# A hybrid decoder step on one core: fetch-aligned TensorE loops, an earlier turn of the next tile, and another bank for the group maps

## The chip, the core and the metric

The kernel runs on one core of a Trainium2 chip. The metric is the device time of one execution in microseconds (us), the median over several runs. TensorE (PE in the rows; PEld is its loading of weights) multiplies, VectorE (DVE) and ScalarE (ACT) do elementwise work, GpSimd (POOL) issues the indirect DMAs and SyncE (SP) most of the others. Each engine has a sequencer that runs its own stream of instructions (PEldq in the rows is TensorE's). Matrix products accumulate in eight banks of PSUM, here `ps[:, 0..7, :]`.

## What is computed

One layer over 1,024 prompt tokens and 64 sample tokens, all in float32, D = 1024:

```python
h = rmsnorm(x, norm1_g)
proj = h @ w_in                                  # u, v, p: 512 columns each
u, v = gelu(proj[..., :512]), layernorm(gelu(proj[..., 512:1024]))
p = proj[..., 1024:]
ya = u * (tril(W_s[h]) @ v_chunk + b[h])         # 4 heads, chunks of 128 tokens
yb = (window_mean(p, 2/4/8/16) - p) @ b_w[g] * b_scale   # 4 groups of 128
x = x + concat(ya, yb) @ w_out
h2 = rmsnorm(x, norm2_g)
eidx, gates = hier_route(h2, ...)                # best of 4 groups, then 2 of its 8 experts
x = x + moe_ffn(h2, eidx, gates, w1, w3, w2)     # 32 SwiGLU experts, 1024 -> 512 -> 1024
y = rmsnorm(x, normf_g)
```

## The kernel before

**The trunk.** `pipeline` runs `step(i, cur, prev, pprev, nxt)` over nine tiles of 128 tokens (i = 0 to 8; the last, "sample", has 64). Steps 2 to 6 are a hardware loop, the others are written out. Every engine has its own `step`, and semaphores tie them together; within an engine the order is the order of the code. On TensorE a step makes these things in a row: the v products (L1249, bank 2), the p products (L1258, bank 4), the u products (L1258, bank 3), the spatial products z (L1274, bank 5), the turn (transposition) of the next tile's normalised `xn` into banks 0 and 1 (L1199), the group maps `bw` of the pooling branch (L1308, bank 6), the turn of the tile before for the router (L1199, banks 0 and 1 again), the first half of the output product (L1326, bank 6), the router's logits (L1334), the second half (L1342, bank 7). `hT` is what VectorE makes of the next tile's turn (`take_hT`, L842): it scales banks 0 and 1 into SBUF. It may only do so when the p and u products, which read the old `hT`, are done, and the router's turn waits for it, since it writes the same banks. `xT_done`, `hT_ready`, `yaT_ready`, `ybT_ready` and `yb_done` are the semaphores in between: `yT` has the four heads' part ("ya") in its first four slices and the groups' part ("yb") in its last four.

On VectorE a step adds the output halves of the tile before, normalises, makes `v`, the pooled sums `poolT` (`pool_tile`), then adds the bias to z (L1010), multiplies by u (L1014, gives `yaT_ready`), makes `hT` (L842), and scales the maps (L1031, gives `ybT_ready`). In step 7 (`LAST - 1`) TensorE also turns the last 15 rows of the pooling input into bank 4 (L1280) and ScalarE copies them out (L726, gives `rows_copied`).

**The experts.** 32 blocks, one an expert, in triples: `triples` writes out the first three blocks (the first triple), then runs a hardware loop for triples 1 to 6 (block sizes 96, 80, 64 tokens), a second loop for triples 7 to 9 (80, 80, 64), and writes out the last two blocks. A block of TensorE (`block_triple`) has 128 products with the two up matrices, four chunks of weights of 1 MB each (L1372, 256 records in the trace, each with a weight load of its own), the turn of the next block's rows (L1199, 8 records), and eight products with the down matrix, two chunks (L1393, 16 records). SyncE loads each chunk of a later triple into the place of the chunk that TensorE has just used (`used`, L470); 18 chunks are held, so a load is asked for one triple ahead. Both loops lie behind one another in TensorE's instruction stream with one register instruction between them; line 346 is the loop's own control on each engine.

TensorE's instructions are fetched in blocks of 256 (16 KB); in the trace they are the packets of DMA queue q8, the instruction queue.

Of the kernel before, what the change touches and what calls it, by code (L numbers as in the profile page):

```python
# [14 lines left out]
P = 128  # L15
# [8 lines left out]
HEADS = GROUPS = 4  # L24
STATE = 15
WINDOWS = (2, 4, 8, 16)
HALO = 16
NG, NE, EPG = 4, 32, 8
NR = NG + NE
FE = 512  # L30
# [35 lines left out]
def reached(eng, sem, n):  # L66

    if not isinstance(n, int) or n > 0:
        eng.wait_ge(sem, n)
# [7 lines left out]
def build(nc, x_prompt, x_sample, state_pool, norm1_g, w_in, a_norm_g, a_norm_b, ws_sht, bs_th,  # L77
# [4 lines left out]
    with ctx:  # L82
# [253 lines left out]
        def m_of(kind):  # L336
            return NS if kind == "sample" else P
# [4 lines left out]
        def triples(eng, block_triple):  # L342

            block_triple(0, (CAP,) * SETS)
            for lo, hi, caps_of in CLASSES:
                with eng.Fori(lo, hi) as h:
                    block_triple(h, caps_of)
            block_triple(FINAL, FINAL_CAPS)
# [459 lines left out]
        def _(dve):  # L808
# [29 lines left out]
            def take_hT(i, m):  # L838
                dve.wait_ge(xT_done, i + 1)
                reached(dve, proj_p, i)  # L840
                reached(dve, proj_u, i)
                dve.tensor_tensor(hT[:, :, 0:m], wide[:, :, 0:m],  # L842
                                  g1t[:, :].unsqueeze(2).to_broadcast([P, KD, m]), ALU.mult)\
                    .then_inc(hT_ready, 1)
# [87 lines left out]
            def step(i, cur, prev, pprev, nxt):  # L932
# [73 lines left out]
                    dve.wait_ge(share_step, 7)  # L1006
                if cur and cur != "sample":
                    pool_tile(i, cur == "first")
                    dve.wait_ge(z_done, i + 1)
                    dve.tensor_tensor(ya[:, :], ps[:, 5, :], bias.rearrange("p h n -> p (h n)"), ALU.add).then_inc(z_biased, 1)  # L1010
                    dve.wait_ge(z_biased, i + 1)
                    dve.wait_ge(u_gelu, i + 1)
                    reached(dve, out_b, i)
                    dve.tensor_tensor(yT[:, 0:HEADS, :], ya.rearrange("p (h n) -> p h n", n=P),  # L1014
                                      u.rearrange("p (h n) -> p h n", n=P), ALU.mult).then_inc(yaT_ready, 1)
                if cur == "sample":
# [5 lines left out]
                        last = dve.scalar_tensor_tensor(ya[0:m, c], ps[0:m, 5, c], bst_s[0:m, h:h + 1],  # L1022
                                                        u[0:m, c], ALU.add, ALU.mult)
                    last.then_inc(ya_ready, 1)
                if nxt:
                    take_hT(i + 1, m_of(nxt))
                if cur:
                    m = m_of(cur)
                    dve.wait_ge(yb_done, i + 1)
                    reached(dve, out_b, i)  # L1030
                    dve.tensor_tensor(yT[:, HEADS:KD, 0:m],  # L1031
                                      ps[:, 6, :].rearrange("p (g n) -> p g n", n=P)[:, :, 0:m],
                                      bsc[:, :].unsqueeze(2).to_broadcast([P, GROUPS, m]), ALU.mult)\
                        .then_inc(ybT_ready, 1)
                if prev:
# [158 lines left out]
        def _(pe):  # L1194
            def turn(x, m, done, k=KD, bank=0, whole=False):

                xs = x[0:m, :].rearrange("t (k p) -> t k p" if whole else "t (p k) -> t k p", k=k)
                for c in range(k):
                    last = pe.transpose(ps[:, bank + c // 4, (c % 4) * P:(c % 4) * P + m], xs[:, c, :],  # L1199
                                        ident[0:m, 0:m])  # L1200
                last.then_inc(done, 1)
# [25 lines left out]
            def step(i, cur, prev, pprev, nxt):  # L1227
# [9 lines left out]
                if cur:  # L1237
                    m = m_of(cur)
                    pe.wait_ge(hT_ready, i + 1)
                    if cur == "sample":  # L1240
                        pe.wait_ge(rows_copied, 1)
                        half_tile_projections(i)
                    else:
                        reached(pe, v_gelu, i)
                        reached(pe, logits_ready, i - 1)
                        for k in range(KD):
                            if isinstance(i, int) and i == 0 and k % 2 == 0:
                                pe.wait_ge(in_win[k // 2], 16)
                            last = pe.matmul(ps[:, 2, :], hT[:, k, :], win[:, k, AW:2 * AW],  # L1249
                                             start=(k == 0), stop=(k == KD - 1))  # L1250
                        last.then_inc(proj_v, 1)
                        for bank, part, free, done in ((4, 2, p_copied, proj_p), (3, 0, u_gelu, proj_u)):
                            reached(pe, free, i)
                            for j in range(AW // P):
                                for k in range(KD):
                                    for c in range(SPLIT):
                                        at = part * AW + j * P + c * NS
                                        last = pe.matmul(ps[c * NS:(c + 1) * NS, bank, j * P:(j + 1) * P],  # L1258
                                                         win[:, k, at:at + NS], hT[:, k, :], start=(k == 0),
                                                         stop=(k == KD - 1), skip_group_check=True)  # L1260
                            last.then_inc(done, 1)
# [21 lines left out]
                    if cur == "sample":  # L1283
# [7 lines left out]
                                                     src[0:kk, g * P + c * w:g * P + (c + 1) * w], bnd[0:kk, g, 0:m],  # L1291
                                                     start=(n == 0), stop=(n == 1), skip_group_check=True)
                        last.then_inc(pooled, 1)
                if nxt:
                    pe.wait_ge(xn_ready, i + 2)
                    reached(pe, h2T_ready, i - 1)
                    turn(xn, m_of(nxt), xT_done)
                if cur:
                    m = m_of(cur)
                    if cur == "sample":  # L1300
                        pe.wait_ge(ya_ready, 1)
                        turn(ya, m, yaT_done, HEADS, 5, whole=True)
                    pe.wait_ge(poolT_ready, i + 1)
                    reached(pe, x2a_ready, i)
                    w = P // SPLIT if cur == "sample" else P
                    for g in range(GROUPS):
                        for c in range(P // w):
                            last = pe.matmul(ps[c * w:(c + 1) * w, 6, g * P:g * P + m], bw[:, g, c * w:(c + 1) * w],  # L1308
                                             poolT[:, g, 0:m], start=True, stop=True, skip_group_check=True)
                    last.then_inc(yb_done, 1)  # L1310
                if prev:
# [4 lines left out]
                if cur:  # L1316
                    m = m_of(cur)
                    if isinstance(i, int) and i == 0:
                        pe.wait_ge(in_wout, 32)
                    pe.wait_ge(yaT_ready, i + 1)  # L1320
                    pe.wait_ge(ybT_ready, i + 1)
                    if cur == "sample":
                        half_tile_output(range(2))
                    else:
                        for k in range(KD):
                            last = pe.matmul(ps[0:m, 6, :], yT[:, k, 0:m], wout[:, k, 0:512],  # L1326
                                             start=(k == 0), stop=(k == KD - 1))
                        last.then_inc(out_a, 1)
# [173 lines left out]
```

## Time and profile before

| | us |
|---|---|
| median of 3 runs | 975.38 (974.15 to 977.6) |
| profiled execution | 981.15 |
| its span, first to last instruction | 979.4 |
| TensorE busy | 888.5 (91%) |
| VectorE busy | 280.8 (29%) |
| TensorE, trunk (to the last router product) | 8.3 to 386.1 |
| TensorE, experts | 390.7 to 943.6 |
| final norm and output behind it | to 979.4 |

The mean granted clock of TensorE over the span was 0.964 of full speed. A row of a timeline has the start in us from the span's start, how long the group lasted, the engine, the source line, the operation, its tiles and shapes, how often, and in brackets the idle time before it and what ended it. "issue" there means that nothing the profile shows was waited for.

### The profile page before, as it was taken

The numbers are of one execution on the slowest core, as the hardware profiler recorded it, in microseconds if no ns is written. First come the engines' busy times: TensorE is split into PE (matmuls) and PEld (weight loads), VectorE is DVE, ScalarE is ACT, GpSimd is POOL, SyncE is SP. The second block draws the span as 40 slices with busy tenths as digits, with TensorE's granted clock in tenths as the row PEclk, the third lists the DMA queues.
The fourth block names the chain that finished last, engine by engine and source line by source line (L and its number), as shares of the span: only waits on it lengthen the run. The fifth ranks groups of instructions, "written<-read, shape, count | busy, mean of one in ns | idle before, by whom it ended". The sixth has DMA issues, their size and how long they took to land. (4 is left out here: it accounts for less than half of the span.)

```text
span 979.4 us, 28026 instructions
## 1 busy us (share of the span) xinstructions
PE 888.5 (91%) x12186; PEld 641.1 (65%) x12186; DVE 280.8 (29%) x838; ACT 100.9 (10%) x158; POOL 155.3 (16%) x262
## 2 busy tenths in 40 slices
PE   4899999999999994999999899997999999999940
PEld 2766848667585762778677576776676767777630
DVE  2544555645556355330101001010010101010106
ACT  0110100101001011010010000000101010101014
POOL 1000100000000002122131302221221322222110
PEclk9999999999999996899999899999999999999985
DMA  9770210201011047999999999999999999999628
GB/s 336 260 271 1 88 39 4 86 0 43 21 64 44 3 140 274 398 400 377 370 399 396 395 370 378 409 389 406 359 396 403 392 407 392 406 395 405 249 68 321
DMA packets 57407, 258.42 MB, mean 264 GB/s; under 512 B 10633, under 2 KB 11713, under 8 KB 40436
## 3 DMA queue, kind: packets, MB, share of 16 engines
q1 hardware_dynamic: 47436, 237.98, 60.9%
q0 software_dynamic: 9264, 19.36, 8.0%
q8 instruction: 56, 0.92, 0.4%
q10 hardware_dynamic: 640, 0.07, 0.1%
q14 instruction: 11, 0.09, 0.0%
HBM read 240.33 MB, written 25.04 MB: 271 GB/s over the span
## 5 line engine op out<-in xcount | busy, mean ns | idle before, releaser
L1372 PEld LDWEIGHTS ps<-hT,big 128*64 128x64 f32 x8192 | 300.1, 139 | 47.1 <-issue 44.7
L1372 PE MATMUL ps<-hT,big 128*64 128x80 f32 (+2 forms) x8192 | 309.8, 236 | 18.2 <-issue 15.1
L1393 PE MATMUL ps<-big,poolT 128*80 128x512 f32 (+2 forms) x512 | 191.2, 594 | 0.6 <-issue 0.6
L1146 DVE TENSOR_TENSOR poolT<-u,ps 128x320 f32<-128x320 f32 (+2 forms) x32 | 15.6, 486 | 427.1 <-PE ps L1372 427.1
L1393 PEld LDWEIGHTS ps<-big,poolT 128*80 128x80 f32 (+2 forms) x512 | 64.5, 150 | 103.1 <-issue 102.0
L1258 PEld LDWEIGHTS ps<-hT,big 128*64 128x64 f32 x2048 | 111.6, 137 | 6.1 <-issue 6.1
L1258 PE MATMUL ps<-hT,big 128*64 128x128 f32 x2048 | 113.6, 273 | 0.0
L584 POOL DMA_INDIRECT x_rows<-xn,sidx x22 | 32.7, 1487 | 278.1 <-ACT xn L782 268.3
L561 POOL DMA_INDIRECT slot_table<-ids,dest x18 | 18.8, 1042 | 300.6 <-DVE dest L899 297.5
L1249 PE MATMUL ps<-big,hT 128*128 128x512 f32 x128 | 58.9, 611 | 4.2 <-DMA big<-in_w_in 2.8
L1326 PE MATMUL ps<-big 128*128 128x512 f32 x128 | 56.4, 593 | 2.1 <-DVE big L1031 2.1
L1342 PE MATMUL ps<-big 128*128 128x512 f32 x128 | 57.0, 598 | 0.0
L782 ACT ACTIVATE xn<-ps,gslot 80x1024 f32<-80x1024 f32 (+1 forms) x21 | 23.3, 1110 | 260.1 <-PE ps L1393 247.8
L1249 PEld LDWEIGHTS ps<-big,hT 128*128 128x128 f32 x128 | 24.3, 195 | 33.4 <-issue 26.7
L1326 PEld LDWEIGHTS ps<-big 128*128 128x128 f32 x128 | 23.7, 190 | 29.2 <-issue 29.0
L1342 PEld LDWEIGHTS ps<-big 128*128 128x128 f32 x128 | 23.7, 190 | 27.6 <-issue 27.3
L1199 PE MATMUL ps<-ident,xn 128*128 128x128 f32 (+1 forms) x144 | 20.5, 289 | 18.6 <-DVE xn L836 8.3
L1063 DVE TENSOR_TENSOR hT<-ps,g2t 128x768 f32<-128x768 f32 (+1 forms) x32 | 28.0, 875 | 27.6 <-PE ps L1199 18.8
L579 POOL DMA_INDIRECT gslot<-gate_rows,pidx x32 | 32.2, 1007 | 21.1 <-POOL sidx L630 13.3
L1199 PEld LDWEIGHTS ps<-ident,xn 128*128 128x128 f32 (+1 forms) x144 | 18.0, 194 | 20.0 <-issue 15.2
L584 POOL DMA_INDIRECT x_rows<-bands,sidx x10 | 14.6, 1460 | 92.6 <-DVE bands L1153 79.4
L703 ACT ACTIVATE xn<-big 128x1024 f32 (+2 forms) x9 | 9.5, 1057 | 171.9 <-DVE big L969 171.9
(202 smaller groups left out, 564.8 us busy)
## 6 DMA issues: line engine op xcount, KB each, us to landing
big<-in_exp_w SPq DMA_DIRECT2D x192, 1024.0 KB, 11.1
big<-in_w_in SPq DMA_DIRECT2D x4, 1536.0 KB, 12.7
big<-in_w_out SPq DMA_DIRECT2D x2, 2048.0 KB, 16.3
x_rows<-big SPq DMA_DIRECT2D x8, 512.0 KB
h_rows<-xn SPq DMA_DIRECT2D x8, 512.0 KB, 2.9
big<-x_rows SPq DMA_DIRECT2D x8, 512.0 KB, 6.9
out_y_prompt<-big SPq DMA_DIRECT2D x8, 512.0 KB, 2.8
big<-in_x_prompt SPq DMA_DIRECT2D x1, 3072.0 KB, 11.2
```

The costliest lines, as they stand in the source:

```text
L561: pool.indirect_dma_start(slot_table, bass.IndirectOffsetOnAxis(ap=dest[0:m, j, c:c + 1], axis=0), ids[0:m, j, c, :], None, bounds_check=N ...
L579: pool.indirect_dma_start(dst, None, gate_rows, bass.IndirectOffsetOnAxis(ap=idx.bitcast(U32), axis=0), bounds_check=last_pair, oob_is_err ...
L584: pool.indirect_dma_start(x3_rows, bass.IndirectOffsetOnAxis(ap=idx.bitcast(U32), axis=0), src, None, bounds_check=last_row, oob_is_err=Tr ...
L782: act.activation(ys[s][0:m, :], ps[0:m, 5:7, :].rearrange("p a n -> p (a n)"), ACT.Copy, scale=gslot[s][0:m, 0:1]).then_inc(y_ready, 1)
L1063: dve.tensor_tensor(xT[:, :, 0:ways * i].rearrange("p k (w i) -> p k w i", i=i), wide.rearrange("p k (i w) -> p k w i", w=WAYS)[:, :, 0:wa ...
L1199: last = pe.transpose(ps[:, bank + c // 4, (c % 4) * P:(c % 4) * P + m], xs[:, c, :], ident[0:m, 0:m])
L1249: last = pe.matmul(ps[:, 2, :], hT[:, k, :], win[:, k, AW:2 * AW], start=(k == 0), stop=(k == KD - 1))
L1258: last = pe.matmul(ps[c * NS:(c + 1) * NS, bank, j * P:(j + 1) * P], win[:, k, at:at + NS], hT[:, k, :], start=(k == 0), stop=(k == KD - 1 ...
L1326: last = pe.matmul(ps[0:m, 6, :], yT[:, k, 0:m], wout[:, k, 0:512], start=(k == 0), stop=(k == KD - 1))
L1342: last = pe.matmul(ps[0:m, 7, :], yT[:, k, 0:m], wout[:, k, 512:D], start=(k == 0), stop=(k == KD - 1))
L1372: last = pe.matmul(out[c * w:(c + 1) * w, j, 0:m], up_weights(n)[:, k, j * P + c * w:j * P + (c + 1) * w], xT[:, 4 * half + k, 0:m], start ...
L1393: last = pe.matmul(ps[first:first + m, 5 + cols, :], hhT[:, 2 * half + k, 0:m], down_weights(n)[:, k, cols * 512:(cols + 1) * 512], start= ...
```

## The change

Three edits. First, on TensorE alone each of the two expert loops begins on a boundary of 256 instructions; the space to the boundary is filled with NOPs, which are executed on the way in (none is skipped by a branch). Second, the turn of the next tile stands between the p and the u products, and on VectorE `take_hT` stands ahead of the bias and the product with u. Third, the group maps of the full tiles go to bank 4, not 6 (which takes a wait for `rows_copied` in step 7), and the first half of the output product waits for `ybT_ready` only ahead of its fifth slice.

```diff
+FETCH_BLOCK = 256
...
             for lo, hi, caps_of in CLASSES:
+                if eng is nc.tensor:
+                    eng.addr_align(FETCH_BLOCK)
                 with eng.Fori(lo, hi) as h:
                     block_triple(h, caps_of)
...
                     pool_tile(i, cur == "first")
+                    if nxt:
+                        take_hT(i + 1, m_of(nxt))
                     dve.wait_ge(z_done, i + 1)
...
-                if nxt:
-                    take_hT(i + 1, m_of(nxt))
...
-                                      ps[:, 6, :].rearrange("p (g n) -> p g n", n=P)[:, :, 0:m],
+                                      ps[:, 6 if cur == "sample" else 4, :].rearrange("p (g n) -> p g n", n=P)[:, :, 0:m],
...
                         for bank, part, free, done in ((4, 2, p_copied, proj_p), (3, 0, u_gelu, proj_u)):
+                            if bank == 3 and nxt:
+                                pe.wait_ge(xn_ready, i + 2)
+                                reached(pe, h2T_ready, i - 1)
+                                turn(xn, m_of(nxt), xT_done)
                             reached(pe, free, i)
...
-                if nxt:
-                    pe.wait_ge(xn_ready, i + 2)
-                    reached(pe, h2T_ready, i - 1)
-                    turn(xn, m_of(nxt), xT_done)
...
+                    maps = 6 if cur == "sample" else 4
+                    if isinstance(i, int) and i == LAST - 1:
+                        pe.wait_ge(rows_copied, 1)
...
-                            last = pe.matmul(ps[c * w:(c + 1) * w, 6, g * P:g * P + m], bw[:, g, c * w:(c + 1) * w],
+                            last = pe.matmul(ps[c * w:(c + 1) * w, maps, g * P:g * P + m], bw[:, g, c * w:(c + 1) * w],
...
                     pe.wait_ge(yaT_ready, i + 1)
-                    pe.wait_ge(ybT_ready, i + 1)
                     if cur == "sample":
+                        pe.wait_ge(ybT_ready, i + 1)
                         half_tile_output(range(2))
                     else:
                         for k in range(KD):
+                            if k == HEADS:
+                                pe.wait_ge(ybT_ready, i + 1)
                             last = pe.matmul(ps[0:m, 6, :], yT[:, k, 0:m], wout[:, k, 0:512],
```

TensorE in the trunk's loop, from the p products to the first output half, before. A name behind "waits" is a semaphore; `ps<-ident,xn` is a turn.

```order
47 L1258 MATMUL ps<-hT,big 64x128 [waits p_copied]
48 L1258 MATMUL ps<-hT,big 64x128 x63
49 L1258 MATMUL ps<-hT,big 64x128 [waits u_gelu]
50 L1258 MATMUL ps<-hT,big 64x128 x63
51 L1274 MATMUL ps<-done_early,v 128x128 [waits rank_taken,v_ready]
52 L1274 MATMUL ps<-done_early,v 128x128 x3
53 L1295 REGISTER_ALU
54 L1199 MATMUL ps<-ident,xn 128x128 [waits h2T_ready,xn_ready]
55 L1199 MATMUL ps<-ident,xn 128x128 x7
56 L1308 MATMUL ps<-poolT,done_early 128x128 [waits x2a_ready,poolT_ready]
57 L1308 MATMUL ps<-poolT,done_early 128x128 x3
58 L1199 MATMUL ps<-ident,xn 128x128 [waits hT_ready,x2n_ready]
```

The same place on TensorE in the changed kernel (its lines are numbered 3 to 8 higher).

```order
53 L1265 MATMUL ps<-hT,big 64x128 x63
54 L1257 REGISTER_ALU
55 L1202 MATMUL ps<-ident,xn 128x128 [waits h2T_ready,xn_ready]
56 L1202 MATMUL ps<-ident,xn 128x128 x7
57 L1265 MATMUL ps<-hT,big 64x128 [waits u_gelu]
58 L1265 MATMUL ps<-hT,big 64x128 x63
59 L1281 MATMUL ps<-done_early,v 128x128 [waits rank_taken,v_ready]
60 L1281 MATMUL ps<-done_early,v 128x128 x3
61 L1314 MATMUL ps<-poolT,done_early 128x128 [waits x2a_ready,poolT_ready]
62 L1314 MATMUL ps<-poolT,done_early 128x128 x3
63 L1202 MATMUL ps<-ident,xn 128x128 [waits hT_ready,x2n_ready]
```

The eight transpositions of the next tile stand ahead of the 64 u products, and between z and the router's turn only the four group maps are left.

VectorE in the same loop, before: bias, product with u, `hT`, scaling of the maps.

```order
212 L1010 TENSOR_TENSOR big<-ps,gf 128x512 [waits z_done]
213 L1014 TENSOR_TENSOR big<-big,u 128x512 [waits out_b,u_gelu,z_biased]
214 L842 TENSOR_TENSOR hT<-ps,g1t 128x1024 [waits proj_u,proj_p,xT_done]
215 L1031 TENSOR_TENSOR big<-ps,bsc 128x512 [waits out_b,yb_done]
```

VectorE there in the changed kernel.

```order
212 L845 TENSOR_TENSOR hT<-ps,g1t 128x1024 [waits proj_u,proj_p,xT_done]
213 L1015 TENSOR_TENSOR big<-ps,gf 128x512 [waits z_done]
214 L1019 TENSOR_TENSOR big<-big,u 128x512 [waits out_b,u_gelu,z_biased]
```

`hT` stands first, and the two operations that make the heads' part of `yT` come behind it.

## Rows read from the trace of the kernel before

**Rows 1.** TensorE's waits: line waited for: us in total, times, longest.

```profile
PE ps L1199 <- DVE hT L842: 5.8, 6, 1.0
```

**Rows 2.** Timeline of TensorE, tile 3, maps and router's turn.

```profile
163.37 1.06 PE L1308 MATMUL ps<-poolT,done_early 128*128 128x128 f32 x8
165.38 1.13 PE L1199 MATMUL ps<-ident,xn 128*128 128x128 f32 x8 [0.96 <-DVE hT L842]
```

**Rows 3.** Timeline of VectorE, tile 3: next tile's norm, bias, product, hT.

```profile
146.82 0.75 DVE L836 TENSOR_SCALAR xn<-big,ss 128x1024 f32 x1 [0.17 <-DVE ss L827]
...
162.69 0.69 DVE L1010 TENSOR_TENSOR big<-ps,gf 128x512 f32<-128x512 f32 x1 [4.21 <-PE ps L1274]
163.41 0.69 DVE L1014 TENSOR_TENSOR big<-big,u 128x512 f32<-128x512 f32 x1
164.02 1.22 DVE L842 TENSOR_TENSOR hT<-ps,g1t 128x1024 f32<-128x1024 f32 x1
```

**Rows 4.** Timeline of TensorE, tile 0: p and u products, maps, output.

```profile
23.50 14.19 PE L1258 MATMUL ps<-hT,big 128*64 128x128 f32 x256
...
40.57 1.16 PE L1308 MATMUL ps<-poolT,done_early 128*128 128x128 f32 x8 [0.91 <-DVE poolT L928]
43.82 7.11 PE L1326 MATMUL ps<-big 128*128 128x512 f32 x16 [2.09 <-DVE big L1031]
```

**Rows 5.** Timeline of VectorE, tile 0: norm of tile 1.

```profile
30.69 0.75 DVE L836 TENSOR_SCALAR xn<-big,ss 128x1024 f32<-128x1024 f32 x1
```

**Rows 6.** Timeline of TensorE, tile 7: maps and router's turn without a wait.

```profile
330.13 1.16 PE L1308 MATMUL ps<-poolT,done_early 128*128 128x128 f32 x8
331.12 1.08 PE L1199 MATMUL ps<-ident,xn 128*128 128x128 f32 x8
```

**Rows 7.** Timeline of ScalarE, tile 7: the copy that gives rows_copied.

```profile
329.27 0.59 ACT L726 ACTIVATE xg<-ps 16x512 f32<-16x512 f32 x1 [1.52 <-PE ps L1280]
```

**Rows 8.** Windows of the experts: stretch, length, busy us (records), PEclk, DMA share, GB/s.

```profile
551.46:574.82 23.36, 17.98 (x274) 14.99 (x273) 1.65 (x2) 1.17 (x2) 4.00 (x6) 0.78 1.02 401
502.50:516.64 14.14, 14.14 (x273) 11.74 (x273) 1.65 (x2) 1.17 (x2) 4.03 (x6) 1.00 1.02 399
659.89:681.34 21.45, 16.39 (x274) 13.24 (x273) 1.65 (x2) 1.17 (x2) 4.01 (x6) 0.92 1.02 406
...
599.89:609.88 9.99, 8.54 (x258) 7.95 (x257) 0.00 (x0) 1.49 (x2) 4.05 (x6) 1.00 1.02 378
650.24:658.81 8.57, 8.31 (x258) 7.86 (x257) 0.00 (x0) 1.49 (x2) 4.02 (x6) 1.00 1.02 383
706.45:716.15 9.70, 8.58 (x257) 8.01 (x256) 0.00 (x0) 1.49 (x2) 4.04 (x6) 1.00 1.03 380
```

**Rows 9.** Loop control of TensorE's sequencer, whole run: ns min/median/max, first and last start.

```profile
L346 PEldq COMPARE_BRANCH  x9: 76/222/7127, 502.6 to 909.9; - x9
...
L346 PEldq MOVE  x2: 29/32/34, 448.7 to 766.5; - x2
```

**Rows 10.** The same control at 551 to 553 us.

```profile
L346 PEldq ALU_OP  x1: 32/32/32, 551.5 to 551.5; - x1
L346 PEldq COMPARE_BRANCH  x1: 7127/7127/7127, 551.6 to 551.6; - x1
```

**Rows 11.** Instruction packets, 506 to 555.1 us (triple 2): packets, MB, share.

```profile
q8 instruction: 1, 0.02, 0.2%
```

**Rows 12.** The same from 555.1 to 614.4 us (triple 3).

```profile
q8 instruction: 8, 0.13, 0.9%
```

**Rows 13.** Timeline of TensorE: first products of triples 1, 3 and 7.

```profile
455.74 10.78 PE L1372 MATMUL ps<-hT,big 128*64 128x96 f32 x256
...
559.08 4.10 PE L1372 MATMUL ps<-hT,big 128*64 128x96 f32 x47 [3.97 <-issue]
...
769.72 9.48 PE L1372 MATMUL ps<-hT,big 128*64 128x80 f32 x256
```

**Rows 14.** SyncE's chunk loads, 866 to 890 us: issue to landing.

```profile
DMA to landing us min/median/max: 25.1/25.1/25.1
```

## The prediction

> **What bounds the kernel now.** Read TensorE's line first: it is busy 91% of the span, so what counts is where it waits and what it executes. Its list of waits names one wait that recurs in the trunk, on `hT`, six times and 5.8 us in all [rows 1]. In the experts it has no large wait with a releaser at all; what is left there is called "issue". The timeline shows where: 3.97 us of nothing ahead of the first product of triple 3 [rows 13], and no such gap at the start of triple 2. Windows laid from the down products of one triple to the first turn of the next give 14.14 us into triple 2, 23.36 into triple 3 and 21.45 into triple 5 [rows 8]. The records are the same (273 or 274), so 9.2 and 7.3 us are pure loss. Part is idle time and part a slow TensorE: the granted clock is 0.78 and 0.92 of full in these windows, against 1.00.
>
> The sequencer's rows say what the gap is. Its nine loop branches take 222 ns in the median, the worst 7,127 ns [rows 9]; that one starts at 551.6 us [rows 10] and ends at 558.7, just ahead of the product at 559.08. The queue of instruction packets fits: one packet in all of triple 2, eight in triple 3 [rows 11, 12]. So triple 2 ran from instructions that were still there, and triple 3 had to fetch its body again, its first block at the branch itself, while TensorE ran dry.
>
> **Why it alternates.** A triple is 3 x (256 + 8 + 16) = 840 products, each with a weight load: 1,680 instructions, and some 13 for control and waits, 1,693 or 6.6 blocks of 256. In triple 3 the products stop again after 47 [rows 13]: 94 instructions and about four others, so the loop's head lies some 98 instructions short of a boundary. 98 + 6 x 256 = 1,634, so 59 more lie in an eighth block. I take it that eight blocks are kept: when a triple runs wholly from kept ones, the fetch of a ninth at its end drops the first, and the back edge misses. Then all come in again in a row, the last too late as well: the third block of triples 3 and 5 lasts 9.99 and 9.70 us where the same products last 8.57 in triple 4 [rows 8]. Loop 2 is the control. It starts 59 + 1 instructions into that eighth block, so it touches only seven, and its back edges are among the seven branches that don't stall [rows 9].
>
> **The loops aligned.** From a boundary, 1,693 instructions touch seven blocks, with the next one eight. What goes: 9.2 + 7.3 us at the two back edges and 1.4 + 1.1 us in the two third blocks, **19.0 us**. Loop 2 gains nothing, it fits already.
>
> What comes is the padding, executed once at each entry: about 98 + 4 = 102 NOPs ahead of loop 1 (the trunk's edits take a few wait instructions out in front of it) and 1,792 - 1,693 - 1 = 98 ahead of loop 2. They hide behind the down products queued in TensorE. At loop 1 the sequencer is at the head at 448.7 us [rows 9], TensorE needs the next product at 455.74 [rows 13], and from a branch's end to the product took 559.08 - 558.7 = 0.4 us: cover 6.7 us. At loop 2 it is there at 766.5, needed at 769.72 (a block of 64 tokens has half as long down products): cover 2.8 us. No NOP is in the trace. The floor is a register move's own 32 ns [rows 9], the ceiling the 100 ns from the start of one control instruction to the next, 551.5 to 551.6 [rows 10], which has the recording of it in it. I take 60 ns, nearer the floor since in the timed runs nothing is recorded. Loop 1: 6.1 us, hidden. Loop 2: 5.9 us, of which 3.1 us TensorE idles, and I add 1.2 us for a clock that may drop after it: the gap of 3.97 and a second of 1.41 us came with 9.2 us of loss, so 3.8 us beyond idling. **Cost 4.3 us.** At 32 ns: 3.3 and 3.1 us, cost 0.3. At 100 ns: 3.5 + 7.0 us idle and twice 3.8, cost 18.1.
>
> **A rule that speaks against this.** The branch that ends triple 1 took some 0.2 us and the one that ends triple 2 took 7.1 [rows 9, 10], with one packet in triple 2 [rows 11]; so a jump of 1,693 instructions back can find its target. The Trainium skill ("Runtime: NRT & Kernel Launch", "Instruction fetch mechanics") says that a taken branch whose target lies outside a window of two pages forces a fetch before execution goes on. By that rule every back edge of both loops would stall in both kernels, and the aligning would bring nothing; the trace disagrees at seven of nine branches. It is a rival below.
>
> **The turn moved ahead of the u products.** The eight transpositions are the same in number, so only the wait goes. From the maps to the router's turn is 165.38 - 163.37 = 2.01 us in tile 3 [rows 2] and 331.12 - 330.13 = 0.99 where nothing is waited for [rows 6]: 1.0 us a tile. `xn` is ready at 147.6 [rows 3], and the p products end at about 154.4, so the turn doesn't wait in the loop. The new order on VectorE: `hT` can start when the u products end, about 162.5 on the shifted clock, and takes 1.2 us; then bias and product, 0.72 and 0.69 us from start to start and end [rows 3], done at 165.2. TensorE's maps and router's turn are through at 165.4. So the output product finds `yT` ready by 0.2 us; if the chain is that much longer, as much comes back. I count 0.95 us, and the wait occurs six times: **5.7 us**. The scaling of the maps is now late, but the output product asks for it only at its fifth slice, 1.8 us on.
>
> Tile 0: p ends at 23.50 + 7.1 = 30.6 [rows 4], `xn` of tile 1 comes at 31.4 [rows 5], so the moved turn waits 0.8 us. It is given back: the maps waited 0.91 us for `poolT` anyway and start where they did, 40.57. Behind them `hT` (1.2), bias and product (1.4) run from 40.6 to 43.2, against 43.82 before: **+0.6 us**. Tile 7: the maps now wait for ScalarE's copy of 0.59 us, which begins 0.1 us after the products it reads [rows 7]; formerly the next tile's turn lay in between and covered it. Maps later by **0.8 us**. Other tiles need no new wait for bank 4: `poolT` is made from what was copied out of it. The trunk is worth 5.7 + 0.6 - 0.8 = **5.5 us**, and since TensorE leads into the routing chain, everything behind it comes as much earlier.
>
> **Is anything late next?** The weights. SyncE loads a chunk when its predecessor is used; in triple 9 it took 25.1 us to land [rows 14], with the DMA engines full [rows 8]. If all 19 us that the stalls gave the queue are added, 44.1 us; it is needed one triple (47.4 us) less its own use (2.7 us) later, 44.7. It fits even then, and the queue was partly idle in the stalls, so the true figure is lower.
>
> **Sum.** 19.0 - 4.3 + 5.5 = 20.2 us. The profiled execution, 981.15, goes to 961.0; the runs' median lies 5.8 us below it, so **955.2 us**.
>
> **Rivals.** (1) Dear NOPs, at or near 100 ns: gain 19.0 + 5.5 - 18.1 = 6.4, **969.0 us**; for it, the only spacing that the trace has; against it, that spacing includes recording. (2) The aligning does not cure the misses, by the two-page rule or since the head doesn't land where it should: the trunk's 5.5 less 0 to 4.3 for the NOPs, **970 to 974 us**. Against it: loop 2. (3) The weights bind in triple 9 and the last two blocks: the margin above is 0.6 us at its worst, and a miss would cost some 3 us, **958 us**. (4) Slower: the NOPs alone decide. With both covers used up (9.5 us) and 7.6 us of slow clock, 200 NOPs cost 200c - 1.9 us; over 24.5 + 2.9 us, that is from c = 0.146 us on. At 0.16 us each the kernel takes 30.1 - 24.5 = 5.6 us longer, **981 us**. A move's own 32 ns speaks against it.
>
> **How the numbers follow.** Forecast 0.66 (951 to 961, both ends from the NOP's price), dear NOPs 0.14, no cure 0.10, weights 0.07, slower 0.03. The range takes in forecast, weights and nearly all of the dear NOPs: low 949.5 (NOPs free, 24.5 us, and 1.4 us less in the first pass of loop 1, whose third block, too, fetches), high 968. About 0.3%, 2.9 us, is what a measurement can tell from no change: faster 0.93 (the no-cure case lies at or under 972.5 in six cases of ten), same 0.04, slower 0.03.
>
> **What would show it.** Right: all loop branches of TensorE near 0.2 us; no instruction packets in triples 3 to 6; windows of 14.1 us into triples 3 and 5; clock 1.00 through the experts; router's turn 1.0 us behind the maps. The gap at 769.72 on the new clock prices the NOP. Wrong: a branch of microseconds, a gap over 4 us at loop 2 or any at loop 1, an output product that waits for the product with u, or products of the last triple that wait for a chunk.

## The result, and the profile after

The changed kernel takes 960.18 us (median of four runs, 958.86 to 961.16) against 974.76 us of the kernel before in the same comparison: ratio 0.9846 with a 95% interval of 0.9819 to 0.9873, 1.5% or about 15 us faster. The forecast was 955.2 us, in a range of 949.5 to 968. The profiled execution took 959.59 us, 957.9 of it its span, with a mean granted clock of 0.967.

The long back edges are gone. TensorE's sequencer rows for the loop's own line (min, median and max duration in ns), which answer to [rows 9]:

```profile
L349 PEldq ALU_OP  x9: 32/32/32, 501.4 to 888.7; - x9
L349 PEldq COMPARE_BRANCH  x9: 76/208/233, 501.5 to 888.9; - x9
```

The worst of nine branches takes 233 ns, where it was 7,127. The windows into triples 2, 3 and 5, then the third block of triple 3 (length, busy time of each engine, clock, DMA share, GB/s), answer to [rows 8]:

```profile
501.60:515.79 14.19, 14.19 (x274) 11.79 (x273) 1.69 (x3) 1.17 (x2) 4.03 (x6) 1.00 1.02 397
549.18:563.33 14.15, 14.15 (x274) 11.75 (x273) 1.65 (x2) 1.17 (x2) 4.01 (x6) 1.00 1.02 398
...
644.72:658.86 14.14, 14.14 (x273) 11.74 (x273) 1.65 (x2) 1.17 (x2) 4.01 (x6) 1.00 1.03 394
592.61:600.23 7.62, 7.62 (x138) 5.35 (x136) 1.38 (x2) 0.01 (x1) 2.36 (x4) 1.00 1.03 373
```

All are alike, at full clock, and TensorE is busy from end to end. The queue of instruction packets moves 39 in all (56 before), and none between 502.2 and 751.9 us; the DMA groups of the page and its row for the weights:

```profile
q8 instruction: 39, 0.64, 0.3%
...
big<-in_exp_w SPq DMA_DIRECT2D x192, 1024.0 KB, 21.5
```

A chunk of weights lands 21.5 us after its issue in the median.

The NOPs are in the trace, unlike before, and so have a price. Sequencer rows of the aligning line:

```profile
L348 PEldq NOP  x200: 13/13/13, 445.9 to 747.6; - x100
```

Their starts are 102 from 445.87 to 453.33 and 98 from 740.50 to 747.55: (747.55 - 740.50) / 97 = 72.7 ns from one to the next (73.9 at loop 1), though each lasts 13. TensorE's timeline at the two entries (start, length, engine, line, operation, tiles, count, idle time before):

```profile
445.95 7.03 PE L1401 MATMUL ps<-big,poolT 128*96 128x512 f32 x16
453.97 1.21 PE L1380 MATMUL ps<-hT,big 128*64 128x96 f32 x24 [0.99 <-issue]
...
740.25 3.65 PE L1401 MATMUL ps<-big,poolT 128*64 128x512 f32 x16
748.02 10.78 PE L1380 MATMUL ps<-hT,big 128*64 128x80 f32 x254 [4.12 <-issue]
760.36 0.35 PE L1380 MATMUL ps<-hT,big 128*64 128x80 f32 x2 [1.55 <-issue]
```

At loop 1 TensorE misses the first product by 0.99 us, at loop 2 by 4.12 us. The block behind the second gap takes 10.78 us where one of 80 tokens takes 9.1, since the granted clock is half of full for 3.4 us after it; and its last two products come 1.55 us late, after an instruction packet that moved at 757.8 us. In the trunk, tile 3:

```profile
145.83 7.21 PE L1265 MATMUL ps<-hT,big 128*64 128x128 f32 x128
152.97 1.16 PE L1202 MATMUL ps<-ident,xn 128*128 128x128 f32 x8
154.06 7.21 PE L1265 MATMUL ps<-hT,big 128*64 128x128 f32 x128
161.20 1.16 PE L1281 MATMUL ps<-done_early,v 128*128 128x128 f32 x8
162.19 1.06 PE L1314 MATMUL ps<-poolT,done_early 128*128 128x128 f32 x8
163.08 1.05 PE L1202 MATMUL ps<-ident,xn 128*128 128x128 f32 x8
164.01 6.28 PE L1334 MATMUL ps<-big 128*128 128x512 f32 x14
```

The router's turn stands 0.89 us behind the maps, no longer 2.01 [rows 2]. Tiles 0 and 7:

```profile
31.97 1.16 PE L1202 MATMUL ps<-ident,xn 128*128 128x128 f32 x8 [1.25 <-DVE xn L839]
...
43.69 7.11 PE L1334 MATMUL ps<-big 128*128 128x512 f32 x16 [1.45 <-DVE big L1019]
...
326.82 1.13 PE L1314 MATMUL ps<-poolT,done_early 128*128 128x128 f32 x8 [0.83 <-ACT xg L729]
```

### The profile page after: what moved, and what is told of

Its sections match the earlier page's. It is cut to its first block and busy times, and to the rows that moved or that the text cites. A ratio compares the mean times of both kernels' runs of the same rounds, so it can differ in the third digit from the quotient of the medians.

```text
span 957.9 us, 28219 instructions
## 1 busy us (share of the span) xinstructions
PE 879.2 (92%) x12186; PEld 634.2 (66%) x12186; DVE 280.1 (29%) x838; ACT 100.8 (11%) x158; POOL 155.3 (16%) x262
## 5 line engine op out<-in xcount | busy, mean ns | idle before, releaser
L1380 PEld LDWEIGHTS ps<-hT,big 128*64 128x64 f32 x8192 | 292.5, 139 | 37.0 <-issue 35.4
L1380 PE MATMUL ps<-hT,big 128*64 128x80 f32 (+2 forms) x8192 | 297.9, 235 | 12.5 <-issue 11.5
L1265 PEld LDWEIGHTS ps<-hT,big 128*64 128x64 f32 x2048 | 111.5, 137 | 7.0 <-issue 6.1
L1202 PEld LDWEIGHTS ps<-ident,xn 128*128 128x128 f32 (+1 forms) x144 | 18.0, 194 | 15.8 <-issue 9.5
## 6 DMA issues: line engine op xcount, KB each, us to landing
big<-in_exp_w SPq DMA_DIRECT2D x192, 1024.0 KB, 21.5
```

The lines of the kernel that those rows point to most:

```text
L1380: last = pe.matmul(out[c * w:(c + 1) * w, j, 0:m], up_weights(n)[:, k, j * P + c * w:j * P + (c + 1) * w], xT[:, 4 * half + k, 0:m], start ...
```

## The experiments

The first four ran on one chip, where the kernel before took 973.47 us (median of seven runs, 971.74 to 975.06).

**The kernel before, recorded again.** No edit.

> The kernel before, unchanged, for a second profile of it. In the first, the 64-token blocks of TensorE took 8.6 us where the changed kernel's take 7.6, with three short stops in each, also in triples that fetched no instructions; and the profiled execution was 5.8 us over the median of the runs. If those stops belong to that one recording, this profile shows 64-token blocks of 7.6 us, an execution near 975 us, and the same two long branches (6 to 7 us) ahead of triples 3 and 5. If they belong to the kernel (where its loops lie in the instruction stream), the blocks take 8.6 us again.

Measured: 973.93 us, span 971.8. Windows into triples 3 and 5, and the third block of triple 5:

```profile
552.66:573.81 21.15, 16.47 (x273) 13.41 (x272) 1.65 (x2) 1.17 (x2) 4.00 (x6) 0.92 1.03 404
...
657.40:679.33 21.93, 15.94 (x274) 13.05 (x273) 1.65 (x2) 1.17 (x2) 4.01 (x6) 0.92 1.03 404
...
704.25:713.75 9.50, 7.83 (x257) 7.68 (x257) 0.00 (x0) 1.49 (x2) 4.03 (x6) 1.00 1.02 382
```

Against windows of 14.15 us into triples 2 and 4 of the same trace, the back edges lose 7.0 and 7.8 us; against 7.62 us of the changed kernel the third blocks lose 1.3 and 1.9. Together about 18 us: the misses and their price repeat. Two things differ from the first recording. A block of 64 tokens takes 7.7 us here, not 8.6 [rows 8], and a triple 1.2 us less (609.75 to 657.52 against 611.08 to 660.01 from branch to branch), so that the first recording's span was longer by 7.6 us. And TensorE's clock falls in tile 0, behind the wait of 2.10 us there, so that sixteen products which take 7.11 us at [rows 4] take 8.80:

```profile
43.55 8.80 PE L1326 MATMUL ps<-big 128*128 128x512 f32 x16 [2.10 <-DVE big L1031]
```

**Only the aligning.**

```diff
+                if eng is nc.tensor:
+                    eng.addr_align(FETCH_BLOCK)
```

> Only the aligning of the two loops; the trunk as before. Theory (eight fetch blocks are kept, an aligned triple touches seven): all nine loop branches of TensorE near 0.2 us, no instruction packets in triples 3 to 6, and of the 14.6 us that the whole change brought some 9, so about 966 us. The NOPs, 71 ns each in the changed kernel's trace, cost what they cost there: a gap of 1 us at loop 1 and 4.1 us at loop 2. Rival (the trunk's new order moved the loop's code or relieved the weights, and the aligning does nothing by itself): 975 us, with the long branches still there.

Measured: 965.09 us (963.87 to 966.28), ratio 0.9907 (0.9887 to 0.9926), 9.1 us less by that ratio, 8.4 between the medians. All branches are short (233 ns at most); 197 NOPs run. The gap at loop 2 has the same size, but the half clock behind it lasts 6.8 us here, and in tile 0, too (sixteen products in 10.1 us):

```profile
754.93 11.48 PE L1375 MATMUL ps<-hT,big 128*64 128x80 f32 x254 [4.12 <-issue]
```

So the aligning alone removes some 18 us and returns half of them.

**Only the trunk's edits.** The changed kernel without the two lines above.

> Only the trunk's edits (turn ahead of the u products, hT first on VectorE, maps in bank 4); no aligning. Theory: 5.5 us less than before, about 969.3 us, the expert loops with their long branches ahead of triples 3 and 5 as before. The changed kernel's trace has 0.70 us less a tile than before in tiles 2 to 6 (40.69 against 41.39), not the 0.95 that I counted, and the first router product of tile 8 came 3.6 us earlier: by that rival reading the trunk is worth 3.6 us, 971.2 us.

Measured: 967.37 us (966.57 to 968.98), ratio 0.9931 (0.9913 to 0.9949), 6.7 us less by the ratio, 6.1 between the medians. The misses stay, with their second stop after 49 products now, not 47 (the new order has three instructions fewer in front of the loop, which took 102 NOPs to align, where the old one took 99; its body reaches 56 instructions into the eighth block, not 59):

```profile
553.90 3.92 PE L1378 MATMUL ps<-hT,big 128*64 128x96 f32 x49 [2.73 <-issue]
559.32 5.50 PE L1378 MATMUL ps<-hT,big 128*64 128x96 f32 x128 [1.50 <-issue]
```

9.1 and 6.7 make 15.8; the two parts add up within the intervals. By one pair of traces, the first recording of before and the changed kernel, the trunk's edits bring 3.6 us where the order before didn't lose its clock, and more where it did: the product that ranks the last tile, the end of the trunk, starts at 385.1, 386.5 and 388.3 us in three recordings with the old order, with 0, 3.4 and 6.8 us of half clock in tile 0, and at 381.6 and 381.9 in the changed kernel and this one, with none. None of the eleven recordings with the new order, those below among them, shows a drop in tile 0: their clock stays at 1.00 from about 18 to 357 us at least. TensorE's longest idle time there is 1.4 us now instead of 2.1, which had 0.5 to 1.1 us of idling just ahead of it. That may be the reason, but it isn't shown: it wasn't tried by itself, the first recording idled 0.9 + 2.1 us and kept its clock, and the wait ahead of the moved turn, up to 1.5 us, is new. And four of the eleven lose the clock later instead, for 3.4 us from 357 or 358 us on, which none of the three with the old order does. One of them, the next kernel below, starts its last ranking at 383.2 us. Why it falls there is open.

**The padding jumped over.** `addr_align` may end in a branch to the boundary instead of NOPs.

```diff
-                    eng.addr_align(FETCH_BLOCK)
+                    eng.addr_align(FETCH_BLOCK, max_nops=0)
```

> The changed kernel, but the padding ahead of both loops is jumped over by one branch, so that none of the 200 NOPs is executed. Theory: the NOPs' gaps of 1.0 and 4.1 us and the 3.4 us of half clock behind the second (1.7 us) go, 6 to 7 us, so about 953.5 us. Rival: the jump leaves the blocks that were fetched in order, so the loop's first block must be fetched at the branch itself, as at the long branches of before: 3 to 4 us of gap at each loop, and the kernel stays at 960 or goes to 963 us.

Measured: 956.87 us (956.11 to 960.16), ratio 0.9824 (0.9806 to 0.9842). The two jumps take 1,999 and 288 ns and neither leaves a gap, and the clock stays at 1.00 from 399 to 925 us. But against the ratio of the changed kernel only some 2 us are gained, of the 6 to 7 that the two gaps and the slow clock had cost. TensorE's timeline in the last triples says where they went in the one execution recorded:

```profile
883.56 1.94 PE L1401 MATMUL ps<-big,poolT 128*64 128x512 f32 x8 [1.22 <-DMA big<-in_exp_w]
886.39 1.94 PE L1401 MATMUL ps<-big,poolT 128*64 128x512 f32 x8 [0.90 <-DMA big<-in_exp_w]
888.98 7.33 PE L1380 MATMUL ps<-hT,big 128*64 128x80 f32 x192 [0.65 <-DMA big<-in_exp_w]
897.46 2.43 PE L1380 MATMUL ps<-hT,big 128*64 128x80 f32 x64 [1.16 <-DMA big<-in_exp_w]
```

With one more wait of 0.45 us at 920.25, TensorE waits 4.4 us for weights; the changed kernel's list of waits has none. So the prediction's rival on the weights did come, in this recording, once the NOPs were gone; that their gap had kept TensorE just behind the DMA is my reading. The recorded execution is the slowest of the four (960.16 us, the others 956.11 to 957.25), and its span of 958.0 us is no shorter than the changed kernel's 957.9. It also starts the ranking 1.7 us later, by the clock. So whether the faster three waited as long for weights isn't known.

The next eight ran on a second chip, in two sets. The kernel before spread widely there (975 to 992 us beside the first, 965 to 984 beside the second), so these kernels are compared with one another.

**Loop 1 at 98 instructions behind a boundary, loop 2 left alone.**

```diff
-                if eng is nc.tensor:
-                    eng.addr_align(FETCH_BLOCK)
+                if eng is nc.tensor and lo == 1:
+                    eng.addr_align(FETCH_BLOCK, offset=98, max_nops=0)
```

> The changed kernel with one difference in the loops' place: loop 1 begins 98 instructions behind a boundary of 256 (reached by a jump, no NOPs executed), and loop 2 gets no padding at all; 98 + 1,693 = 1,791, so its head falls on a boundary by itself. Theory (a back edge finds its target as long as the body touches at most seven blocks, wherever it begins): no long loop branch, none over 0.3 us, no instruction packets between 502 and 745 us, and no gap at loop 2, where not even a jump is left: about 957 us, as with the jumps, and with the same waits of TensorE for weights near the end. Rival (the boundary itself matters, a head in mid-block is fetched anew): branches of 6 us or more at triples 3 and 5, 968 us or more.

Measured: 960.17 us (959.71 to 962.05). No long branch in a body that begins in mid-block and fills its seventh block to the end (by the trace the loop's register move stands at the place that is named, and the body one behind it: 99 to 1,791):

```profile
L349 PEldq COMPARE_BRANCH  x9: 76/208/257, 500.7 to 889.9; - x9
```

It isn't the boundary that matters but the number of blocks touched. Of the 957 us and the waits for weights that I expected, neither came; the blocks of 64 tokens are why, below.

**Loop 1 at 104.** `offset=104` for loop 1, and loop 2 brought to a boundary by a jump.

> As the kernel with loop 1 at 98 instructions behind a boundary, but at 104; loop 2 is brought to a boundary by a jump. 104 + 1,693 = 1,797, so the last five instructions of the body lie in an eighth block. Theory (eight blocks are kept, and running into the eighth makes the ninth be fetched over the first): the long branches are back at the ends of triples 2 and 4, 6 to 7 us each, packets of the instruction queue come all through triples 3 and 5, and their windows are 21 to 22 us, not 14.2. 14 to 18 us of that show against the kernel at 98, less up to 4 us which the waits for weights now hide: 967 to 974 us. Rival (only the amount of code beyond the eighth block counts, five instructions set off nothing): no long branch, 957 us.

Measured: 963.3, 973.3, 975.9 and 982.3 us, a spread that the kernel at 98 hasn't. In the recording (975.9) triples 3 and 5 are reached without a miss, against the theory; but the end of triple 5 has the long branch, and all of triple 6 is fetched again:

```profile
L349 PEldq COMPARE_BRANCH  x9: 76/208/6967, 500.9 to 905.1; - x9
```

```profile
695.27 3.65 PE L1401 MATMUL ps<-big,poolT 128*64 128x512 f32 x16
702.73 4.89 PE L1380 MATMUL ps<-hT,big 128*64 128x96 f32 x74 [3.81 <-issue]
...
761.51 2.80 PE L1380 MATMUL ps<-hT,big 128*64 128x80 f32 x38 [4.56 <-issue]
```

Six instructions' difference in place and the miss is back, at one of five back edges where 59 instructions in the eighth block made it two of five. With so few instructions there (six, since the body begins one behind the 104), the ninth block is mostly not asked for before the loop turns back: no packet moves between 498.5 and 698.2 us, over four short back edges, and the next two come at 698.2 and 698.9, behind the long one. That is how I read it; the spread of the four times would fit a count of misses that changes from run to run, but only one run was recorded. The second gap is another loss: the jump to loop 2 took 5,887 ns here.

**Only loop 1 aligned.**

```diff
-                if eng is nc.tensor:
+                if eng is nc.tensor and lo == 1:
```

> The changed kernel with only loop 1 on a boundary (102 NOPs); loop 2 follows where it falls, 159 instructions behind a boundary, and its body of 1,693 reaches 60 instructions into an eighth block. Theory (a body in eight blocks misses at every second back edge): the end of triple 8 has a branch of 6 to 7 us and triple 9 is fetched again; loop 1 has none. Against the changed kernel: -4.1 us for the gap of the NOPs, -1.5 us of slow clock, -2.7 us of first-pass stops, +7 to 8 us for the back edge, +1 to 2 us for the third block: 958.5 to 963.5 us. Rival (loop 2 is too short, with three passes, to miss, and its alignment is a pure cost): no long branch, 952 to 954 us, or 957 if the weights bind.

Measured: 971.17 us (962.21 to 972.9), beyond the 958.5 to 963.5 expected. The changed kernel takes 969.85 on this chip, in the other set below, so that the two differ by 1.3 us, inside the -1.7 to 3.3 us that the expectation makes; with runs that spread over 10.7 us this is weak support. The mechanism came as forecast: loop 2, at 159, has no gap at its entry and one miss, at the end of its second pass.

```profile
L349 PEldq COMPARE_BRANCH  x9: 76/208/7006, 501.9 to 901.4; - x9
```

```profile
746.48 3.65 PE L1401 MATMUL ps<-big,poolT 128*64 128x512 f32 x16
749.97 6.35 PE L1380 MATMUL ps<-hT,big 128*64 128x80 f32 x175
...
843.05 3.65 PE L1401 MATMUL ps<-big,poolT 128*64 128x512 f32 x16
850.55 3.46 PE L1380 MATMUL ps<-hT,big 128*64 128x80 f32 x47 [3.85 <-issue]
855.79 6.41 PE L1380 MATMUL ps<-hT,big 128*64 128x80 f32 x126 [1.79 <-issue]
```

So loop 2 needs its padding only since loop 1 was moved; where it lay before, it didn't miss.

**The 15 rows turned earlier.** As the kernel at 98; in step 7 the turn of the rows stands ahead of the spatial products, so that ScalarE's copy has these to hide behind.

```diff
+                    if isinstance(i, int) and i == LAST - 1:
+                        pe.wait_ge(p_copied, i + 1)
+                        for g in range(GROUPS):
+                            last = pe.matmul(ps[0:HALO, 4, g * P:(g + 1) * P], pT[:, g, P:HALO + P], ident[:, :],
...
+                        last.then_inc(rows_turned, 1)
                     for h in range(HEADS):
```

> As the kernel with loop 1 at 98 and no NOPs, and in step 7 the turn of the 15 rows of the pooling input stands ahead of the spatial products instead of behind them, so that ScalarE's copy of them (0.59 us) runs under these products. Theory: the wait of 0.83 us ahead of the group maps in step 7 goes, and the expert stage begins 0.8 us earlier, but the weights' waits near the end grow by as much or less: 0.2 to 0.8 us less than that kernel, about 956.3 us. Rival (the whole chain behind the maps has slack there, or the weights take all of it): no difference, 957 us.

Measured: 958.31 us (957.97 to 960.69), 1.9 us less than its neighbour, though their ranges overlap, and the same kernel takes 959.95 us in the next set; so the gain in time isn't shown. TensorE's timeline has no wait ahead of the maps:

```profile
323.90 1.05 PE L1279 MATMUL ps<-ident,bands 128*16 128x128 f32 x8
324.88 1.16 PE L1287 MATMUL ps<-done_early,v 128*128 128x128 f32 x8
325.87 1.06 PE L1314 MATMUL ps<-poolT,done_early 128*128 128x128 f32 x8
```

The maps start 0.95 us earlier than in the changed kernel. The last tile's ranking starts at 380.4 to 381.9 us in three recordings with this edit, and at 381.1 to 383.2 in eight with the new trunk and without it.

**The changed kernel, the last version, and both with less to load.** The two kernels with half chunks leave out half of every sixth chunk, in the loops and the last blocks, and make its products with old weights:

```diff
-                    load_chunk(turn[s], n)
+                    if c < CH - 1:
+                        load_chunk(turn[s], n)
+                    else:
+                        sp.dma_start(chunk_dst(n, c)[:, 0:1, :], chunk_src(turn[s], c)[:, 0:1, :]).then_inc(chunk_in[n], 16)
```

> The changed kernel itself once more, as the yardstick of the three beside it: about 960 us, 200 NOPs 72.7 ns apart, the gap of 4.1 us at the head of loop 2, no wait of TensorE for a chunk of weights over 0.5 us.

> The version with jumps instead of NOPs (loop 1 at 98 instructions behind a boundary) and the 15 rows turned ahead of the spatial products, beside the changed kernel on one chip. Without any limit behind it, it should save the gap of 4.1 us, some 1.5 us of slow clock and 0.8 us in step 7: 6.4 us. Theory (the weights take back what exceeds their margin): it saves 2.5 to 4 us, 956 to 957.5 us, and TensorE waits for chunks of weights in the last 50 us of the experts, 2 to 4 us in all, where the blocks of 64 tokens run at their full speed (7.7 us each). Rival (the weights don't bind, the jumps save less than they seem): no such waits and still only 2 to 4 us.

> The same, with only half of every sixth chunk (the second half of the down matrix) loaded in the loops and the last blocks; the products are all still made, on stale weights there, so their results differ. 1/12 less to load, some 3.7 us less a triple for the queue. Theory (weights bind): the waits for chunks go, loads land in well under 25 us at the end, and the kernel is 2 to 4 us faster than with whole chunks: 952.5 to 954.5 us. Rival: no difference from whole chunks.

> The changed kernel with the same half chunks, the control: if its NOP gap keeps TensorE just behind the weights, the smaller loads gain nothing, 0 to 0.7 us, about 960 us. Rival (less traffic makes everything faster, the waits apart): it gains as much as the version with jumps does, 2 to 4 us.

Measured:

| | us | whole chunks to half |
|---|---|---|
| changed kernel | 969.85 (967.96 to 971.1) | |
| with half chunks | 964.77 (964.46 to 966.17) | -5.1 |
| jumps and rows earlier | 959.95 (958.55 to 961.88) | |
| with half chunks | 957.43 (955.77 to 959.37) | -2.5 |

The version with jumps beats the changed kernel by 9.9 us here, with no overlap. The record has both ahead of the kernel before (ratios 0.9776, 0.9715 to 0.9837, and 0.9876, 0.9815 to 0.9937); but the six runs of before lie at 965.0, 974.8 and four times at 982.5 to 984.4, so that its fastest one is above all runs of the version with jumps and below all of the changed kernel. This set can't say that the changed kernel is faster than before; the first comparison does. Their spans differ by 9.0 us: 3.1 lie ahead of the first loop branch (502.94 and 499.84), 0.9 of it already at the start of the experts, and 6.3 between the sixth and the ninth (150.8 and 144.5), where the gap of 4.12 us and 6.8 us at half clock (3.4 us) have gone.

The weights were not decided by this pair. My theory wanted waits of TensorE for chunks, and there are none in any of the four; the half chunks then had nothing of that kind to remove, and what they brought went to the control more than to the test. The rival is nearer to it; in the control the span's 3.6 us are spread, 1.2 ahead of the first loop branch, 1.4 between it and the last one, 1.0 behind. The 1.4 are no more than the clock's part: it is at half for 3.4 us behind the gap, not for 6.8, which makes 1.7. Why there were no waits is in the block of 64 tokens, first of the kernel with jumps on the first chip, then of the version with jumps on the second:

```profile
588.54 7.69 PE L1380 MATMUL ps<-hT,big 128*64 128x64 f32 x256
```

```profile
588.00 8.73 PE L1380 MATMUL ps<-hT,big 128*64 128x64 f32 x256
```

Each such block takes about 1 us longer, in stops of 0.3 us, and a triple 49.0 us instead of 47.8. In the seven whole triples between loop branches that makes 8.8 us (5 x 1.23 and 2 x 1.33), most of the 9.7 between the changed kernel here and in the first comparison. With TensorE 1.2 us slower a triple, the DMA engines keep ahead of it, and the waits of 4.4 us are not there: that fits a margin of the weights that is just used up at full speed, but it is argued from different kernels on different chips, not shown.

## Why the prediction held, point by point

**What bounds the kernel, and why it alternates.** Right. The gaps were the back edges' fetches. A body touching seven blocks never misses, from a boundary or from 98 behind one: nine recordings with seven back edges each, none over 0.26 us. One reaching 56 to 60 instructions into an eighth misses at every second turn, in either loop (four recordings). Where it reaches only six, the theory named the wrong turns and too many.

**The rule that spoke against it.** The Trainium skill ("Runtime: NRT & Kernel Launch", "Instruction fetch mechanics") has a taken branch stall when its target is outside a window of two pages. All seven jumps back of 1,693 instructions took at most 233 ns here (the other two of the nine branches leave a loop, in 76 ns; the prediction counted them in), so the rule doesn't hold for TensorE in these runs. The same section of the Trainium skill gives TensorE's store as 128 KiB, 2,048 instructions, which is the eight blocks of 256 that I took from the trace. The run at 98 agrees with that figure, the one at 104 only in part, with one miss where two were expected.

**The loops aligned, 19.0 us.** Right: 18 to 19. From branch to branch, triples 2 to 6 took 257.7 us in the second recording of before (505.0 to 762.7) and 238.8 in the changed kernel (501.5 to 740.4), 18.9 less.

**The padding, 4.3 us.** This is the term that was too small. The counts, 102 and 98, were exact, but a NOP costs 72.7 ns, not the 60 that I chose between 32 and 100, so that TensorE idles 4.1 us at loop 2, not 3.1; the slow clock was 1.7 or 3.4 us, not 1.2. I had leaned to the low side because nothing is recorded in the timed runs; but the recorded execution, 959.59 us, lies among the four of its kernel, so nothing shows that recording made the NOPs dearer. Two effects weren't in the sum at all. At loop 1 the cover of 6.7 us was short by 1.0 us. And the first pass of each aligned loop stops at its packets more than before: at loop 2 1.55 + 0.54 + 1.28 us, against 0.26 + 0.49 + 1.41 in the second recording of before, and at loop 1 0.35 + 0.43 + 1.48 behind the entry against 1.09. A NOP takes a slot in a packet but feeds no product, so 98 of them run a packet down with TensorE getting nothing; that reading is argued, not shown. In all the padding costs 4.1 + 1.0 + 1.7 + 1.2 + 1.2 = 9.2 us, 4.9 more than forecast. Both gaps that the prediction had named as signs of being wrong came, one over 4 us at loop 2 and one at loop 1, and the clock was not at 1.00 all through the experts.

**The trunk, 5.5 us.** The waits went as said, but the trace gives 3.6. A tile takes 40.69 us instead of 41.39: 0.70, not 0.95, six times. The turn between p and u costs TensorE more than where it stood (15.37 us from the first p product to z, 14.12 without it: 1.25 us, against 0.9 to 1.0 before), and why that is so wasn't looked into. In tile 0 next to nothing came back: the turn waited 1.25 us, not 0.8, and the output product started 0.13 us earlier, not 0.6. Tile 7 lost 0.83, as forecast. What I hadn't seen is the clock of tile 0, which the first recording didn't show: the runs gain 6.7 us by the trunk, since the old order loses 1.7 and 3.4 us there in two recordings of three; that the new one never drops its clock there is seen in eleven recordings, but its cause isn't shown.

**Is anything late next?** Right for the changed kernel, whose weights are never late. But that owes something to luck: in the recording with jumps on the first chip, without the gap of the NOPs in front of it, the margin didn't hold.

**From the profiled execution to the median.** I took 5.8 us off. That recording had its blocks of 64 tokens at 8.6 us, the second one of before and the one of the changed kernel at 7.7. Between these two the spans differ by 971.8 - 957.9 = 13.9 us; 18.9 from the back edges and 4.3 by the start of the experts (391.48 and 387.20, 1.7 of it the clock in tile 0), less 9.2 for the padding, make 14.0. What is left out cancels: only that recording of before has a wait of 2.3 us for rows in its first triple, and the changed kernel loses some 2 us in small pieces before and behind the loops.

So the forecast of 20.2 us became 15: 4.9 us in the padding's price, and in the trunk 1.9 us less by work, 1.7 or more back by the clock. That last part the prediction didn't have; it is luck that it offset the trunk's shortfall.

## What to carry to other kernels

Count the instructions of a loop on its engine and ask in how many fetch blocks it lies, not only how long it is: here seven blocks of 256 turn back in 0.2 us and eight cost 7 to 9 us at every second turn, and a shift of six instructions brought one such miss back. Pad by a jump (one took 5.9 us, so look where its target lies), or choose the place so that the next loop needs none; two hundred NOPs gave back half of what the alignment had won. And when a stall goes, look for what it had been covering: in the recording where the last gap was closed first, the weights were late by 4.4 us.

## What the runs showed of the hardware

- A NOP on TensorE lasts 13 ns in the trace and costs 73 ns from start to start: 72.7 in the four recordings that have NOPs ahead of loop 2, 73.8 to 74.2 in the five that have them ahead of loop 1.
- A jump forward to a loop's head took from 288 to 5,887 ns in six recordings. Both ends are jumps to loop 2: 288 where loop 1 fills seven blocks and the head begins the eighth, 5,887 where it reaches into the eighth and the head begins a ninth.
- Behind idle times of 2 to 5 us, in tile 0 and in the experts, the granted clock often fell to half, for 3.4 to 10.2 us, and the same gap of 4.12 us gave 3.4 in two recordings and 6.8 in two.
- The same kernel runs its blocks of 64 tokens in 7.7 us in some recordings and in 8.6 to 8.7 in others, in stops of 0.3 us with no releaser. Triples without a miss take 47.8 us on the first chip and, but for one, 48.8 to 49.0 on the second. The cause stays open; fewer bytes of weights didn't remove it.
